# Strassen's algorithm for the MLP's up projection too, with the MLP in two phases and its inner combinations kept in DRAM

## The reference

```python
    x = x + gate1 * mixed
    h = rms_norm(x, norm2_g) * (1.0 + scale2) + shift2
    x = x + gate2 * (jnp.square(jax.nn.relu(h @ w_mlp1)) @ w_mlp2)
```

## Time and profile before

| what | us |
|---|---|
| median of 3 runs | 1162.71 |
| lowest and highest | 1159.84, 1163.24 |
| the profiled execution | 1163.36 |
| its span (first to last instruction) | 1160.8 |

### The profile page before, as it was taken

The page is one execution under the profiler, slowest core; times in us unless marked ns, Lnnn a source line. Parts: engine busy times, 40 slices in busy tenths (PEclk is TensorE's granted clock), DMA queues, the critical chain, the costliest instruction groups (busy, mean ns, idle before and its releaser), DMA issues.

```text
span 1160.8 us, 14544 instructions
## 1 busy us (share of the span) xinstructions
PE 1123.7 (97%) x5370; PEld 911.5 (79%) x5370; DVE 745.2 (64%) x1188; ACT 402.0 (35%) x622; POOL 181.7 (16%) x221
## 2 busy tenths in 40 slices
PE   5999999999999999899999999999999999999887
PEld 4678877777778886678888888888888888888676
DVE  5673556665447665986748657667667567576574
ACT  5342344354444343443223142142241331331322
POOL 2011000000002004303103113013022031031212
PEclk9899999999999999999999999999999999999989
DMA  9958433332113013011111211111111111112015
GB/s 269 268 167 260 135 110 109 109 109 73 32 32 126 22 37 100 1 37 55 55 55 38 72 36 54 54 52 48 44 54 55 53 54 54 54 36 68 23 36 145
DMA packets 114108, 92.66 MB, mean 80 GB/s; under 512 B 11621, under 2 KB 106001, under 8 KB 114065
## 3 DMA queue, kind: packets, MB, share of 16 engines
q1 hardware_dynamic: 106000, 63.72, 19.1%
q0 software_dynamic: 8064, 28.36, 7.5%
HBM read 83.68 MB, written 8.39 MB: 79 GB/s over the span
## 4 chain that ended last, share of the span: by engine, by line
PE 92%; DVE 5%; ACT 1%; DMA 1%; issue 1%; SPq 0%; DVEq 0%; ACTq 0%
PE ps L530 28%; PE ps L532 27%; PE ps L531 27%; PE ps L647 1%; PE ps L666 1%; PE ps L658 1%; DMA xin<-in_x_dram 1%; DVE ht L1572 1%; PE ps L590 1%; DVE act_lo L1559 1%; PE ps L768 1%; PE ps L869 1%; PE ps L622 1%; PE ps L572 1%; DVE rinv L1570 1%
## 5 line engine op out<-in xcount | busy, mean ns | idle before, releaser
L1683 DVE SCALAR_TENSOR_TENSOR x1t<-ps,ada,x1t 128x512 f32<-128x512 f32 x224 | 167.8, 749 | 90.0 <-PE ps L532 89.3
L530 PE MATMUL ps<-act_hi,wm_hi 128*128 128x512 f32 x512 | 200.4, 391 | 2.7 <-issue 1.7
L531 PE MATMUL ps<-act_lo,wm_hi 128*128 128x512 f32 x512 | 199.3, 389 | 0.0
L532 PE MATMUL ps<-act_hi,wm_lo 128*128 128x512 f32 x512 | 199.2, 389 | 0.0
L530 PE MATMUL ps<-hb_hi,wm_hi 128*128 128x512 f32 x448 | 175.8, 392 | 9.1 <-DVE wm_lo L1621 9.1
L531 PE MATMUL ps<-hb_lo,wm_hi 128*128 128x512 f32 x448 | 175.0, 391 | 0.0
L532 PE MATMUL ps<-hb_hi,wm_lo 128*128 128x512 f32 x448 | 174.9, 390 | 0.0
L530 PE MATMUL ps<-act_hi,w_hi 128*128 128x512 f32 x400 | 162.3, 406 | 3.0 <-DVE act_lo L1341 3.0
L532 PE MATMUL ps<-act_hi,w_lo 128*128 128x512 f32 x400 | 157.1, 393 | 0.0
L531 PE MATMUL ps<-act_lo,w_hi 128*128 128x512 f32 x400 | 157.0, 392 | 0.0
L530 PEld LDWEIGHTS ps<-act_hi,wm_hi 128*128 128x128 f32 x512 | 96.1, 188 | 25.4 <-issue 2.4
(11 more groups left out here) (192 smaller groups left out, 1546.3 us busy)
## 6 DMA issues: line engine op xcount, KB each, us to landing
wada<-in_w_ada_dram POOLq DMA_DIRECT2D x32, 512.0 KB, 5.2
w_raw<-in_w_mlp_dram SPq DMA_DIRECT2D x32, 512.0 KB, 4.0
raw_d<-in_w_mlp_dram SPq DMA_DIRECT2D x32, 512.0 KB, 3.5
w_raw<-in_w_in_dram SPq DMA_DIRECT2D x18, 512.0 KB, 3.9
ada_rows<-in_w_ada_dram SPq DMA_DIRECT2D x16, 512.0 KB, 7.4
xin<-in_x_dram SPq DMA_DIRECT2D x8, 512.0 KB, 5.0
x_spill<-xt POOLq DMA_DIRECT2D x8, 512.0 KB, 7.2
x1t<-x_spill POOLq DMA_DIRECT2D x8, 512.0 KB, 4.7
```

Source lines behind the costliest of these rows:

```text
L530: pe.matmul(bank, wh, hi, start=first, stop=False, skip_group_check=onto)
L531: pe.matmul(bank, wh, lo, start=False, stop=False, skip_group_check=onto)
L532: return pe.matmul(bank, wl, hi, start=False, stop=last, skip_group_check=onto)
L1683: dve.scalar_tensor_tensor(out=x1t[:, m, HALVES[half]], in0=ps[:, banks[p % 2], :], scalar=ada[:, 5 * KT + m:5 * KT + m + 1], in1=x1t[:, m ...
```

## The change

The whole MLP is now made of 32 pairs, each 7 products of 4 blocks and 3 passes, 84 matmuls. Pairs 0 to 15 (the first phase) are the up projection: weight block i times combination i of the normalised activations, which are made once, between normalisation and first product. The seven products of an up pair leave TensorE in four PSUM banks (X, W, V, Y, two sets for odd and even pairs), and ScalarE (`e1`, `e5`, `e2`) and VectorE (`c11`, `e25`, `c22`, `c12`, `c21`) combine them into the four blocks of the hidden matrix; VectorE squares the positive part of each (`squared`) and forms the down projection's combinations (`hidden_sums`, `last_sum`). SP stores all seven, 256 KB each, to a DRAM tensor `h_spill`. Pairs 16 to 31 (the second phase) are the down projection in 4 chunks of 1024 hidden features. At each chunk the seven combinations, 1 MB each, are loaded again and split (`combination_hi`, `combination_lo`). The matmuls of the MLP go from 2880 (1536 up, 1344 down) to 2688. There is one set of weight slots, 7 blocks each, high and low, freed product by product; the raw weights have two buffers of 1 MB, filled by four DMAs of 256 KB (`load_pair`). No hardware loop is left.

TensorE's order in the first phase is A11 and A12 of the next pair, then S1, S3, S2, S4, A22 of this pair. In the second phase it is 0 to 6, with A22 last.

```diff
-CHUNKS = 8
-CF = FF // CHUNKS
-NP = KT // 2
 HK = KT // 2
+PAIRS = 16
...
+UP_ORDER = (S1, S3, S2, S4, A22)
+SEQUENCE = [(0, A11), (0, A12)]
+for _p in range(PAIRS):
+    if _p + 1 < PAIRS:
+        SEQUENCE += [(_p + 1, A11), (_p + 1, A12)]
+    SEQUENCE += [(_p, _i) for _i in UP_ORDER]
+SEQUENCE += [(_w, _i) for _w in range(PAIRS, 2 * PAIRS) for _i in range(7)]
...
+            def load_pair(w):
+                if w < PAIRS:
+                    q, j = divmod(w, CHUNK_PAIRS)
+                    rows, cols = 0, ((KT * q + j) * P, (KT * q + HK + j) * P)
+                else:
+                    q, j = divmod(w - PAIRS, CHUNK_PAIRS)
+                    rows, cols = KT * q, (2 * j * P, (2 * j + 1) * P)
+                w_k = w1_k if w < PAIRS else w2_k
+                for o in range(2):
...
+                        sp.dma_start(raw_of(w)[o][l][:, :, :],
+                                     w_k[:, rows + HK * l:rows + HK * (l + 1), cols[o]:cols[o] + P]).then_inc(s_rawm[w % 2], 16)
...
+            store_b11(0)
+            for p in range(PAIRS):
+                if p:
+                    store_sums(p - 1)
+                    store_b21(p - 1)
+                sp.wait_ge(s_wlm, SPLIT[p, A22])
+                load_pair(p + 2)
+                if p + 1 < PAIRS:
+                    store_b11(p + 1)
+                if p == PAIRS - 2:
+                    hidden_stored(0)
+                    load_in_place(0, B11)
+                    load_in_place(0, B21)
+                if p == PAIRS - 1:
+                    load_in_place(0, T1)
+                    load_in_place(0, T2)
+                    load_in_place(0, T3)
+                store_b22(p)
...
+            def weight_sum(w, i):
+                (a11, a12), (a21, _) = raw_of(w)
+                out, (s1, s2) = wm_f[:, blocks_of(w, i), :], (wm_f[:, blocks_of(w, s), :] for s in (S1, S2))
+                slot_free(pool, w, i)
+                if i == S1:
+                    raw_loaded(pool, w)
+                    pool.tensor_tensor(out, a21[:, :, :], raw_of(w)[1][1][:, :, :], ALU.add).then_inc(s_s, 1)
+                elif i == S2:
+                    pool.wait_ge(s_s, 4 * w + 1)
+                    pool.tensor_tensor(out, s1, a11[:, :, :], ALU.subtract).then_inc(s_s, 1)
+                elif i == S4:
+                    pool.wait_ge(s_s, 4 * w + 2)
+                    pool.tensor_tensor(out, a12[:, :, :], s2, ALU.subtract).then_inc(s_s, 1)
+                else:
+                    pool.tensor_tensor(out, a11[:, :, :], a21[:, :, :], ALU.subtract).then_inc(s_s, 1)
...
+            def product(w, i, bank, first, part_there=None):
+                a = blocks_of(w, i)
+                pe.wait_ge(s_wlm, SPLIT[w, i])
+                for j in range(HK):
+                    if part_there is not None:
+                        part_there(j)
+                    mm = passes(bank, wm_hi[:, a, :][:, j, :], wm_lo[:, a, :][:, j, :], cmb_hi[i][:, j, :], cmb_lo[i][:, j, :],
+                                first and j == 0, j == HK - 1, not first)
+                mm.then_inc(s_pd, 1)
...
+            for p in range(PAIRS):
+                if p + 1 < PAIRS:
+                    first_products(p + 1)
+                if p >= 2:
+                    pe.wait_ge(s_cd, n_c12(p - 2))
+                product(p, S1, up_bank(p, "V"), True, None if p else normed_sums(0))
+                if p >= 2:
+                    pe.wait_ge(s_cd, n_c21(p - 2))
+                product(p, S3, up_bank(p, "Y"), True, None if p else normed_sums(HK))
+                pe.wait_ge(s_ec, n_e1(p))
+                product(p, S2, up_bank(p, "X"), False, None if p else normed_sums(2 * HK))
+                pe.wait_ge(s_ec, n_e5(p))
+                product(p, S4, up_bank(p, "V"), False, None if p else normed_sums(3 * HK))
+                pe.wait_ge(s_cd, n_c22(p))
+                product(p, A22, up_bank(p, "Y"), False, None if p else normed_sums(4 * HK))
...
+            def c11(p):
+                dve.wait_ge(s_pd, PRODUCT[p, A12])
+                dve.wait_ge(s_ec, n_e1(p))
+                dve.tensor_tensor(stage[:, p % 2, :], up_bank(p, "W"), stage[:, p % 2, :], ALU.add).then_inc(s_cd, 1)
+            def e25(p):
+                dve.wait_ge(s_pd, PRODUCT[p, S2])
+                dve.wait_ge(s_ec, n_e5(p))
+                dve.tensor_tensor(stage[:, ST_B22, :], up_bank(p, "X"), stage[:, ST_B22, :], ALU.add).then_inc(s_cd, 1)
+            def c22(p):
+                dve.wait_ge(s_cd, n_e25(p))
+                dve.tensor_tensor(stage[:, ST_B22, :], up_bank(p, "Y"), stage[:, ST_B22, :], ALU.add).then_inc(s_cd, 1)
+            def c12(p):
+                dve.wait_ge(s_pd, PRODUCT[p, S4])
+                dve.wait_ge(s_ec, n_e2(p))
+                wait(dve, s_stt, 16 * p)
+                dve.tensor_tensor(stage[:, ST_T3, :], up_bank(p, "V"), stage[:, ST_B21, :], ALU.add).then_inc(s_cd, 1)
+            def c21(p):
+                dve.wait_ge(s_pd, PRODUCT[p, A22])
+                dve.tensor_tensor(stage[:, ST_B21, :], up_bank(p, "Y"), stage[:, ST_B21, :], ALU.add).then_inc(s_cd, 1)
...
+            for k in range(HK):
+                sums_f(T1, k)
+                if k < HK - 2:
+                    normed2()
+                if k:
+                    sums_lo(k, T1, k - 1)
+            normed2()
+            sums_lo(HK, T1, HK - 1)
+            normed2()
+            for k in range(HK):
+                sums_f(T3, k)
+                sums_f(T2, k)
+                if k < HK - 2:
+                    normed2()
+                if k:
+                    sums_lo(HK + k, T3, k - 1)
+            weight_lo(0, S3)
+            sums_lo(2 * HK, T3, HK - 1)
+            for k in range(HK):
+                sums_f(NT4, k)
+                sums_lo(2 * HK + k + 1, T2, k)
+            c11(0)
...
+                if p:
+                    weight_lo(p, S4)
+                    weight_lo(p, S3)
+                    weight_lo(p, A22)
+                    if p + 1 < PAIRS:
+                        c11(p + 1)
+                        squared((p + 1) % 2, n_c11(p + 1))
+                        weight_lo(p + 2, A11)
+                        weight_lo(p + 2, A12)
                     else:
+                        both_lo(0, B11)
+                        both_lo(0, B21)
+                e25(p)
+                c22(p)
+                squared(ST_B22, n_c22(p))
+                c12(p)
+                squared(ST_T3, n_c12(p))
+                hidden_sums(p)
+                if p == 0:
+                    weight_lo(2, A11)
+                    weight_lo(2, A12)
+                if p == PAIRS - 1:
+                    both_lo(0, T1)
+                weight_lo(p + 1, S1)
+                weight_lo(p + 1, S2)
+                c21(p)
+                squared(ST_B21, n_c21(p))
+                last_sum(p)
...
+                add_product(w, 0)
+                if pp == 0:
+                    both_lo(q, T3)
+                elif more:
+                    weight_lo(w + 1, A11)
+                add_product(w, 1)
+                if pp == 0:
+                    weight_lo(w + 1, A11)
+                    combination_lo(q, B22, 0)
+                if ends:
+                    both_lo(q + 1, B11)
+                if more and pp:
+                    weight_lo(w + 1, A12)
+                add_product(w, 2)
+                if pp == 0:
+                    combination_lo(q, B22, 1)
+                    weight_lo(w + 1, A12)
+                if ends:
+                    both_lo(q + 1, B21)
+                add_product(w, 3)
+                if pp == 0:
+                    both_lo(q, NT4)
+                add_product(w, 4)
```

More of the change, by code:

```diff
@@ new lines, in _ @@
+            e2(0)
+            weight_hi(2, A11)
+            weight_hi(2, A12)
+            weight_hi(1, S1)
+            weight_hi(1, S2)
+            weight_hi(1, S4)
+            for p in range(1, PAIRS):
+                weight_hi(p, S3)
+                weight_hi(p, A22)
+                if p + 1 < PAIRS:
+                    e1(p + 1)
+                e5(p)
+                if p + 1 < PAIRS:
+                    weight_hi(p + 2, A11)
+                    weight_hi(p + 2, A12)
+                weight_hi(p + 1, S1)
+                e2(p)
+                if p == PAIRS - 1:
+                    combination_hi(0, T1)
+                weight_hi(p + 1, S2)
+                weight_hi(p + 1, S4)
+                if p == PAIRS - 2:
+                    combination_hi(0, B11)
+                    combination_hi(0, B21)
```

802 lines of the change are left out of this document (439 added, 363 removed).

## The result

| | before | changed |
|---|---|---|
| median us (lowest to highest) | 1162.75 (1159.84 to 1163.24), 4 runs | 1173.58 (1171.23 to 1174.5), 4 runs |
| span of the profiled execution | 1160.8 | 1172.6 |
| mean granted clock | 0.990 | 0.979 |

The ratio is 1.0095, 95% interval 1.0073 to 1.0118: slower by 0.9%. The forecast was 1171 in a range of 1148 to 1196.

The account below looks back on a forecast made before the run. TensorE, busy 97% of the span, was taken to bound the kernel. From 1163.4 us, less 43.5 and 12, plus 27, 15, 9 and 12, the sum was 1170.9; the forecast was 1171, range 1148 to 1196.

Parts of the forecast that it names:

- 192 matmuls: MLP on TensorE: 2880 matmuls become 2688, at 0.2267 us each, 43.5 us saved.
- last chunk's wait, half clock, issue: End of the MLP: the 9.08 us wait, 1.8 of half clock and some 1 of loop issue go, together 12.
- ahead of the MLP: Before the first MLP product: TensorE could start it at 476.6, as before; no loss was counted.
- entry: Start of the MLP: TensorE waits for VectorE's instructions after the second half's reciprocal, +27 us (22 to 31).
- ring: Up pairs: VectorE's chain through the weight DMA takes 20.1 us against TensorE's 19.04; 14 pairs, +15 us.
- change of phase: From up to down: VectorE's work delays two TensorE products by 3.9 us each; with meetings +9 (5 to 14).
- chunk changes: Three later chunk changes: VectorE ends late and TensorE waits for additions, 4 us each, +12 (3 to 18).
- meetings: VectorE instructions with both inputs in SBUF, starting during a GpSimd sum, lengthen by up to 1.0 us each.
- rival 2: Up pairs: the VectorE and DMA chain fits under TensorE's 19.04 us per pair, giving 1151; chance 0.25.
- Rival 3: Up pairs: GpSimd sums block VectorE fully, three of 1.29 us per pair, giving 1207 (two: 1190); chance 0.12.
- Rival 4: SP's queue: weight loads land 2 us late behind stores, up-pair chain 22.1 us, +28, giving 1199; chance 0.08.
- The clock: TensorE: half clock where it has work appears in the earlier trace only behind 9 us of idleness.

Follow-up runs that it names:

- e25: Not a run but a code name: a VectorE step of the changed kernel's up pairs that helps combine the seven products into the hidden matrix's four blocks.
- e4: Changed kernel with the early weight splits moved from steps 4 to 9 of the output projection's second pass to steps 7 to 9: 1171.19 us.
- e1: Changed kernel with the low parts of A11 and A12 moved behind `e25`, `c22` and the square of B22: 1157.97 us.
- e2: Changed kernel with the raw loads of A11 and A12 on a semaphore of their own, order and work unchanged: 1157.29 us.
- e5: e1 plus, in the second phase, additions ahead of low parts where a chunk begins, and T2 ahead of T1 at the change of phase: 1161.18 us.
- e3: Changed kernel with GpSimd writing a constant in place of each pair's four weight sums, so the output is wrong: 1138.83 us.
- e8: Changed kernel with a pair's weight loads ahead of the previous pair's stores of sums, B21 and NT4 in SP's queue: 1177.49 us.

## Why the prediction was right, and which terms were not

The direction, the places and the total held; that the total is so near is in part luck. Of the 4.3 us between the two sums in the table, +10.9 and -6.6 stand against each other. I compare spans: 1172.6 less 1160.8 is +11.8, the forecast's sum 1170.9 less 1163.4 is +7.5. "Lost" is the elapsed time of TensorE less 0.2267 for each matmul.

| term | forecast | measured |
|---|---|---|
| 192 matmuls | -43.5 | -43.5 |
| last chunk's wait, half clock, issue | -12 | -12.9 |
| ahead of the MLP | 0 | +4.3 |
| entry | +27 | +27.5 |
| ring | +15 | +17.8 |
| change of phase | +9 | +12.3 |
| chunk changes | +12 | +8.5 |
| behind the last matmul | 0 | -2.2 |
| sum | +7.5 | +11.8 |

**Matmuls.** 192 records fewer, and starts still 0.227 apart. Right.

**Last chunk.** The wait is gone. What no wait explains (8.5 us in the MLP before, 6.5 after) fell by 2.0, where the forecast had 1.

**Ahead of the MLP: the step that was missing.** The forecast let TensorE's first MLP product start where it could before, at 476.6. It started at 480.92, 4.3 us later, mostly through the two waits of 1.9 that e4 removed (in e4 TensorE is free for it at 475.8). I had counted the entry's instructions from the second half's reciprocal on and had not counted the splits ahead of it. That reciprocal ended at 494.5 and not at 488.5, and e4 brings back half of this.

**Entry.** From the reciprocal to the end of `c22` of pair 0 the forecast has 38.4 us; A22 of pair 0, which needs that bank, starts 37.9 us after it, at 532.45. TensorE lost 29.8 from 480.92 to there, and 2.3 more at half clock behind it (the last matmul at 0.63 starts at 536.45): 32.1 against 4.6 before. The 27.5 fit the 27, but by two errors: the first matmul came later, which shortens the wait, and the half clock was not in the sum. The wait for S3's low part is 10.15 (forecast 10). The one ended by L1874 is at A22 of pair 0, where the forecast put another at A11 of pair 2 behind it; that one does not exist: the low part of A11 of pair 2 is done at 536.9, and A22, at half clock, gives way to that product only at 537.47.

**Ring: right in mechanism, 0.3 us short per pair.** 18.8 without meetings was built from 5.95 + 4.04 + 6.1 + 0.7 + 1.3 + 0.72; the chain shows 6.30 + 3.87 + 6.50 + 0.66 + 2.41 + 0.64. The load is longer by 0.4. The meetings cost 1.11 at the two low parts and 0.35 in the squares, 1.46 against the 1.3 taken. They are not where the forecast put them: the first is S2's sum with the low parts of A11 and A12. Thirteen pairs wait and not 14; twelve periods of 20.42 and a first wait of 1.19 make 17.8. e1 and e2 show that this ring is the cause; without it the changed kernel is faster than the kernel before, which is the forecast's rival 2, whose condition (the ring under 19.26) they meet by an edit.

**Rival 3, GpSimd blocking fully.** The mechanism is there, the price was wrong. The timeline of both engines in the same ring:

```profile
692.88 2.39 DVE L1792 TENSOR_TENSOR wm_lo<-raw,wm_hi 128x512 fp32r<-128x512 f32 x2 [5.86 <-ACT wm_hi L1290]
695.19 0.68 DVE L1870 TENSOR_TENSOR stage<-ps,stage 128x512 f32<-128x512 f32 x1
695.91 0.69 DVE L1874 TENSOR_TENSOR stage<-ps,stage 128x512 f32<-128x512 f32 x1
...
693.02 1.71 POOL L655 TENSOR_TENSOR wm_f<-wm_f,raw 128x512 f32<-128x512 f32 x1 [4.15 <-PE ps L691]
695.74 1.27 POOL L658 TENSOR_TENSOR wm_f<-raw,wm_f 128x512 f32<-128x512 f32 x1 [1.01 <-PE ps L691]
```

The first low part runs to 693.44. GpSimd's sum starts at 693.02 and ends at 694.73, which is 693.44 plus the 1.29 of a sum alone. The second low part, the one of 1.78 in the chain, ends at 695.27, 0.54 behind the sum. That is one instruction at a time, each waiting for the other's end. The next sum (695.74, 1.27) runs beside `c22`, which reads PSUM, and neither is longer. So of the three sums in the ring one cost nearly its whole length and the others 0.35 together, where the rival had 1.29 each. Where VectorE has both inputs in SBUF while a sum runs, as in the row of 4.53 us of e5, two sums cost 2.2 us, which is near the rival's price. The Trainium skill's page "SBUF — State Buffer" (the section "Who interferes with whom") says that a VectorE instruction with two SBUF inputs contends with a GpSimd instruction that reads SBUF, not with one that only writes it; it calls the ports that the two share an exclusive lock, where the order of issue decides who blocks. These rows agree, and so does e3: beside constant writes the low parts take 706 ns in place of 850.

**Rival 4, loads behind stores.** The load of the ring shown took 6.50 us in all, not over 7.5, and e8 moved the stores without gain.

**Change of phase.** Forecast two waits of 3.9, and one or two meetings. Measured 2.04 + 0.88 and 7.00, and 1.5 at half clock behind the last and 0.9 of small losses. The first was too high, the second too low; its releaser is an addition (L1991), as forecast for S3. By e5 the two are one debt of VectorE: reordering moved it and didn't shorten it.

**Chunk changes.** Two waits (1.23 + 1.01) and 0.3 us at each restart (the first matmul behind such a wait lasts 0.50 in place of 0.39), 79.01 us for four pairs of 76.17: 2.8 each, forecast 4. The two places named, S2's product and a later one, are right; the meetings were fewer than the 12 to 14 open instructions allowed. e3 shows that without them nothing would be waited for.

**The clock.** The forecast said the trace shows half clock only behind 9 us of idleness. In the changed kernel it is there behind 3.97, 6.46 and 7.00 too, 1.5 to 2.3 us each, and this was in no term.

**Behind the last matmul.** The span goes on for 7.3 us before (from 1153.5) and 5.0 after (from 1167.55). No run bears on why; it stays open.
